# Six of eight memory-key slabs issued between the chunk inverse's levels and the state products, and RWKV's gate multiplied in by GpSimd

## The reference, cut to what matters

```python
y = wkv7_scan(rh, decay, kh, vh, -kk, kk * ah)       # 8 heads of 64, state 64 x 64 per head
y = head_group_norm(y, gn_w, gn_b, GN_EPS_RWKV)      # per head and token
bonus = jnp.sum(rh * kh * r_k, axis=-1, keepdims=True) * vh
return (y + bonus) * g                               # g: the gate
...
x = x + concat([y_ret, y_rwkv]) @ w_out
k, v = jnp.split(rmsnorm(mem, norm_mem) @ w_kv, 2, axis=-1)   # memory: 256 tokens
```

## Time and profile before

| | us |
|---|---|
| median of 3 runs (1261.39 to 1266.18) | 1261.75 |
| profiled execution, span | 1263.4 |
| TensorE (PE) busy | 1228.3 |
| VectorE (DVE) busy | 681.6 |
| ScalarE (ACT) busy | 552.0 |
| GpSimd (POOL) busy | 530.2 |

### The profile page before, as it was taken

One profiled execution on the slowest core, in us unless ns is written; L12 is line 12 of the kernel. 1 busy time (PEld: TensorE's weight loads), 2 busy tenths in 40 slices (PEclk: granted clock), 3 DMA queues, 4 the chain that ended last, 5 costly groups with the idle time before them and its releaser, 6 DMA issues.

```text
span 1263.4 us, 20863 instructions
## 1 busy us (share of the span) xinstructions
PE 1228.3 (97%) x8361; PEld 994.7 (79%) x8361; DVE 681.6 (54%) x821; ACT 552.0 (44%) x749; POOL 530.2 (42%) x245
## 2 busy tenths in 40 slices
PE   9999999877999999999999999999999999999997
PEld 5887777777878877888888888888787777887876
DVE  8877558776595432463152141344678765443832
ACT  5444553434534333532132231235343478885342
POOL 4333327303576422744444444446443332333453
PEclk9999999999999999999999999999999999999998
DMA  7552212100373210323332233222422421122231
GB/s 266 187 167 85 67 63 72 53 4 5 103 232 101 82 52 34 117 84 100 100 100 88 96 101 100 100 88 96 155 87 84 124 69 64 54 67 71 96 100 67
DMA packets 35099, 119.40 MB, mean 95 GB/s; under 512 B 4544, under 2 KB 4800, under 8 KB 34624
## 3 DMA queue, kind: packets, MB, share of 16 engines
q1 hardware_dynamic: 30624, 106.19, 25.2%
q10 hardware_dynamic: 4384, 11.93, 3.0%
HBM read 110.50 MB, written 2.10 MB: 89 GB/s over the span
## 4 chain that ended last, share of the span: by engine, by line
PE 82%; DVE 11%; ACT 3%; issue 3%; DMA 0%; POOL 0%; DVEq 0%; POOLq 0%; SPq 0%; ACTq 0%
PE banks L1455 22%; PE banks L1457 22%; PE banks L1456 22%; PE banks L1950 1%; PE banks L1966 1%; PE banks L2064 1%; PE banks L2049 1%; DVE a_lo L877 1%; DVE vv L869 1%; DVE yk L869 1%; PE banks L1478 1%; PE banks L1524 1%; PE banks L1480 1%; PE banks L1479 1%; DVE a_lo L869 1%
## 5 line engine op out<-in xcount | busy, mean ns | idle before, releaser
L386 POOL TENSOR_TENSOR w_lo<-w_raw,w_hi 128x1024 fp32r<-128x1024 f32 x144 | 352.0, 2445 | 509.4 <-ACT w_hi L443 509.3
L443 ACT ACTIVATE w_hi<-w_raw 128x1024 fp32r<-128x1024 f32 x144 | 152.7, 1061 | 318.5 <-PE banks L1457 213.5
L1457 PE MATMUL banks<-a_hi,w_lo 128*128 128x512 f32 x608 | 237.1, 390 | 0.0
L1455 PE MATMUL banks<-a_hi,w_hi 128*128 128x512 f32 x576 | 228.6, 397 | 1.8 <-DVE a_lo L869 1.8
L1456 PE MATMUL banks<-a_lo,w_hi 128*128 128x512 f32 x576 | 224.4, 390 | 0.0
L1457 PE MATMUL banks<-b_hi,w_lo 128*128 128x512 f32 x384 | 149.5, 389 | 0.0
L869 DVE TENSOR_TENSOR x_res<-banks,x_res 128x512 f32<-128x512 f32 x62 | 42.9, 691 | 177.7 <-PE banks L1457 174.2
L1457 PEld LDWEIGHTS banks<-a_hi,w_lo 128*128 128x128 f32 x608 | 114.2, 188 | 24.2
L386 POOL TENSOR_TENSOR w_lo<-w_raw,w_hi_mlp 128x1024 fp32r<-128x1024 f32 x36 | 87.3, 2424 | 109.1 <-ACT w_hi_mlp L443 109.1
L1455 PEld LDWEIGHTS banks<-a_hi,w_hi 128*128 128x128 f32 x576 | 108.2, 188 | 30.3 <-issue 4.9
L1456 PEld LDWEIGHTS banks<-a_lo,w_hi 128*128 128x128 f32 x576 | 108.3, 188 | 21.4 <-issue 0.2
(11 more groups left out here) (392 smaller groups left out, 2332.4 us busy)
## 6 DMA issues: line engine op xcount, KB each, us to landing
w_raw<-in_weights SPq DMA_DIRECT2D x188, 512.0 KB, 3.3
x_in<-in_x SPq DMA_DIRECT2D x4, 512.0 KB, 7.8
decay<-in_decay ACTq DMA_DIRECT2D x1, 2048.0 KB, 7.7
rot<-raw SPq DMA_DIRECT2D x32, 64.0 KB, 2.7
x_res<-in_x ACTq DMA_DIRECT2D x4, 512.0 KB, 4.4
consts<-in_consts SPq DMA_DIRECT2D x1, 1093.0 KB, 11.8
q_twice<-q_twice ACTq DMA_DIRECT2D x8, 128.0 KB, 2.8
k_stack<-qk_lo ACTq DMA_DIRECT2D x8, 128.0 KB, 2.6
```

The source lines that it names most:

```text
L386: nc.gpsimd.tensor_tensor(o, a, b, op).then_inc(S(name), 1)
L443: return nc.scalar.activation(o, a, f, **kw)
L1455: mm(o, high[:, w], hi[:, kc, :], start=kc == first, stop=False)
L1457: done = mm(o, w_lo[:, s % 4, w], hi[:, kc, :], start=False, stop=kc == last)
```

## The change

TensorE runs key slabs 0 to 3 after the `next_x` of levels 0 to 3, slab 4 after `chunk_states` and slab 5 after `transitions` (`memory_slab`), slabs 0 to 4 into bank 7 and slab 5 into bank 0. To free bank 7, two f share a pair of banks in the levels (`level_pair`, `level_place`), the transposes go to banks 4, 5, 6 and 4 (`turn_bank`), and `chunk_states(3)` shares banks with f = 2. ScalarE copies each early slab unscaled to SBUF (`memory_taken`); VectorE scales the six later, after `mem_v`. Slabs 2 and 3 have w_hi slots of their own (`w_hi_early`). The splits of the memory and of the slabs move ahead to match.

GpSimd multiplies the gate into the biased bonus (behind w_lo of slab 3) and into the RWKV output (behind w_lo of value slab 1); ScalarE scales by gn_w in its copy; VectorE adds the two (`gated_bonus`). The head sums come after slab 7, the spreads after value slabs 2 and 3. `mixer_lo` of the retention half moves ahead, and the first two W_OUT slabs run their first four chunks before either runs its last four.

```diff
 # GpSimd, behind w_lo of slab s
+                if s == S_MK + 3:
                     for f in range(NF):
-                        pool.wait_ge(S("r_copied"), f + 1)
-                        mul(QT[:, f, :], QT[:, f, :], rx[:, f, :], "qt_ready", ALU.add)
+                        pool.wait_ge(S("bonus_biased"), f + 1)
+                        mul(bon[:, f, :], bon[:, f, :], gx[:, f, :], "rwkv_gated")
+                if s == S_MK + 4:
                     for kc in range(1, KC):
...
+                if s == S_MK + 5:
+                    for f in range(NF):
+                        pool.wait_ge(S("r_copied"), f + 1)
+                        mul(QT[:, f, :], QT[:, f, :], rx[:, f, :], "qt_ready", ALU.add)
+                if s == S_MV + 1:
+                    for f in range(NF):
+                        pool.wait_ge(S("head_sq_ready"), NF + f + 1)
+                        mul(yk[:, f, :], yk[:, f, :], gx[:, f, :], "rwkv_gated")
 # ScalarE
+            def memory_taken(k):
+                act.wait_ge(S("slab_done"), S_MK + k + 1)
+                actv(mem_raw(k), early_bank(k), copy).then_inc(A("tile_taken"), 1)
...
+            for kc in range(KC):
+                memory_hi(kc)
             for lv in range(4):
+                if lv > 0:
+                    memory_taken(lv - 1)
                 for f in range(NF):
                     turned(NF * (lv + 1) + f)
-                memory_hi(2 * lv)
-                memory_hi(2 * lv + 1)
+                split_hi(S_MK + 2 + lv)
+                if lv in (1, 2):
+                    bonus_bias(2 * lv - 2)
+                    bonus_bias(2 * lv - 1)
...
-                actv(yk[:, f, :].rearrange("p (t u c) -> p u t c", u=2, c=CH), y, copy).then_inc(A("act_step"), 1)
+                actv(yk[:, f, :].rearrange("p (t u c) -> p u t c", u=2, c=CH), y, copy, scale=V("gn_w", f)).then_inc(A("act_step"), 1)
...
+            for c in range(KC):
+                split_hi(S_MV + 2 + c)
...
+            for f in range(NF):
+                act.wait_ge(S("y_ready"), f + 1)
+                actv(a_hi[:, NF + f, :], yk[:, f, :], copy).then_inc(A("a_hi_ready"), 1)
 # VectorE
                 for f in range(NF):
-                    dve.wait_ge(S("nx_done"), NF * lv + f + 1)
-                    tt(turned_slots(ak_tile(f, 0)), chunks(pair(f)), mask, ALU.mult).then_inc(D("px_ready"), 1)
+                    dve.wait_ge(S("nx_done"), NF * lv + 2 * (f // 2) + 2)
+                    tt(turned_slots(ak_tile(f, 0)), chunks(level_pair(f)), mask, ALU.mult).then_inc(D("px_ready"), 1)
...
-                if 1 <= lv < 4:
-                    memory_lo(2 * lv - 2)
-                    memory_lo(2 * lv - 1)
+                if lv == 0:
+                    for kc in range(KC):
+                        memory_lo(kc)
...
+            for c in range(NF):
+                mixer_lo(c)
             dve.wait_ge(S("mem_rms"), 1)
             recip(mem_rs[:], mem_rs[:]).then_inc(D("dve_step"), 1)
-            for n in range(KC):
+            for n in range(EARLY, KC):
...
+            for f in range(NF):
+                head_norm2(f)
+            gated_bonus(0)
+            gated_bonus(1)
+            mixer_lo(NF)
+            gated_bonus(2)
+            mixer_lo(NF + 1)
+            gated_bonus(3)
+            mixer_lo(NF + 2)
+            mixer_lo(NF + 3)
...
+            for k in range(EARLY):
+                step(tt(mem_k[:, k, :], mem_raw(k), mem_rs[:], ALU.mult))
 # TensorE
             for lv in range(4):
                 for f in range(NF):
-                    pe.wait_ge(S("px_ready"), NF * lv + f + 1)
+                    pe.wait_ge(S("px_ready"), NF * lv + 2 * (f // 2) + 2)
                     pe.wait_ge(S("xt_ready"), NF * lv + f + 1)
                     x_px(f)
                 for f in range(NF):
                     pe.wait_ge(S("xn_ready"), NF * lv + f + 1)
-                    turn(f, 2 * f)
+                    if lv == 0 or f == NF - 1:
+                        pe.wait_ge(S("xt_ready"), NF * (lv + 1) + 1 if f == NF - 1 else NF)
+                    turn(f, turn_bank(NF + f))
                 for f in range(NF):
-                    pe.wait_ge(S("xt_ready"), NF * (lv + 1) + f + 1)
+                    pe.wait_ge(S("xn_ready"), NF * lv + 2 * (f // 2) + 2)
                     next_x(f)
+                memory_slab(lv)
...
+            memory_slab(4)
             for f in range(NF):
-                pe.wait_ge(S("bc_ready"), f + 1)
+                pe.wait_ge(S("bc_ready"), f + 1 + (f == 2))
...
+            pe.wait_ge(S("r_copied"), 1)
+            memory_slab(5)
...
+            pe.wait_ge(S("heads_normed"), 3 * NF)
+            for n in range(2):
+                begin(S_WOUT + n)
+                part(S_WOUT + n, a_hi, a_lo, range(NF), "a_lo_ready" if n == 0 else None, KC)
+            for n in range(2):
+                part(S_WOUT + n, a_hi, a_lo, range(NF, KC), "a_lo_ready" if n == 0 else None, KC).then_inc(S("slab_done"), 1)
+            for n in range(2, KC):
+                slab(S_WOUT + n, a_hi, a_lo)
```

More of the change, by code:

```diff
@@ L324, in state, with mem_raw, early_bank, level_pair @@
             return ak_tile(f, 0)[:, 0, 0, :] if c == 1 else ST[:, c, f, :]
+        def mem_raw(k):
+            return mem_first[:, k, :] if k < 2 else mem_next[:, k - 2, :]
+        def early_bank(k):
+            return psum[EARLY_BANK[k]][:, 0:MEM]
+        def level_pair(f):
+            return pair(f // 2, f % 2)
+        def level_place(r, half, n, f):
+            return place(2 * (f // 2) + r, half, n, f % 2)
+        def turn_bank(n):
+            return 2 * n if n < NF else TURN_BANK[n % NF]
+        def state_pair(f):
+            return pair(2, 1) if f == NF - 1 else pair(f)
         def solved(f, u):
@@ L1722, in next_x @@
                                 r, t = slice(CH * p, CH * p + CH), 2 * tp + u
[L1723 removed]
+                                last = mm(level_place(p, u, 2 * h + tp, f), ABR[r, f, h, t, 0, :], X[r, f, h, t, :], start=True, stop=True)
                 last.then_inc(S("nx_done"), 1)
@@ L1764, in chunk_states @@
                             r = slice(CH * p, CH * p + CH)
-                            mm(place(2 * f + p, h, t), ABR[r, f, h, t, 2, :], GH[r, 2 * f + h, t, 1, :], start=True, stop=False)
+                            mm(place(bank + p, h, t, k), ABR[r, f, h, t, 2, :], GH[r, 2 * f + h, t, 1, :], start=True, stop=False)
                     for p in range(2):
@@ L1768, in chunk_states @@
                             r, e = slice(CH * p, CH * p + CH), (2 * f + h) * HD
-                            last = mm(place(2 * f + p, h, t), k_tok[r, t, e:e + HD], v_tok[r, t, e:e + HD], start=False, stop=True)
+                            last = mm(place(bank + p, h, t, k), k_tok[r, t, e:e + HD], v_tok[r, t, e:e + HD], start=False, stop=True)
                 last.then_inc(S("bc_done"), 1)
@@ L1779, in transitions, with memory_slab @@
                             last = mm(o, GH[r, 2 * f + h, t, 0, :], ABR[r, f, h, t, 1:3, :], start=True, stop=True)
-                last.then_inc(S("at_done"), 1)
+                last.then_inc(S("bc_done"), 1)
+            def memory_slab(k):
+                s, o = S_MK + k, early_bank(k)
+                high = hi_slot(s)[0]
+                pe.wait_ge(S("w_lo_ready"), s + 1)
+                if 0 < k < 5:
+                    pe.wait_ge(S("tile_taken"), S_MK + k)
+                for kc in range(KC):
+                    if k == 0:
+                        pe.wait_ge(S("mem_lo_ready"), kc + 1)
+                    w = slice(kc * P, (kc + 1) * P)
+                    mm(o, high[:, w], mem_hi[:, kc, :], start=kc == 0, stop=False)
+                    mm(o, high[:, w], mem_lo[:, kc, :], start=False, stop=False)
+                    last = mm(o, w_lo[:, s % 4, w], mem_hi[:, kc, :], start=False, stop=kc == KC - 1)
+                last.then_inc(S("slab_done"), 1)
             def y_inputs(f):
@@ L1941, in slab_and_sums @@
                 part(s, b_hi, b_lo, range(KC - 2, KC), "b_lo_ready", KC * k).then_inc(S("slab_done"), 1)
-            for n in range(KC):
-                slab(S_WOUT + n, a_hi, a_lo, "a_lo_ready" if n == 0 else None, KC)
+            pe.wait_ge(S("heads_normed"), 3 * NF)
[6 more added lines that the diff above has]
+                slab(S_WOUT + n, a_hi, a_lo)
             def xscores(h):
```

131 lines of the change are left out of this document (69 added, 62 removed).

## The result

| | before | changed |
|---|---|---|
| median of 20 runs each, us | 1263.38 (1260.14 to 1266.18) | 1265.30 (1262.96 to 1267.25) |
| ratio, 95% interval | | 1.0018 [1.0011, 1.0025] |
| the same pair on a second chip, us | 1264.41 (23 runs) | 1264.03 (12 runs), 1.000 [0.9986, 1.0013] |
| profiled execution, span, us | 1263.4 | 1264.8 |

The change costs 0.18% on the first chip and nothing on the second: no difference of 0.5%, as the likeliest case had it, but on the other side of no change (+1.9 us where -1.9 was forecast), and 0.3 us above the range.

A forecast was written before the change was run, and what follows sets the result against it. TensorE, carrying 82% of the last chain, was the bound, so only its waits could be won. Running shift: +13.8 us by `y_inputs`, -6.3 after slabs 6 and 7, -6.1, -3.6 at W_OUT slab 2, +1.7 clock: -1.9, 1259.9; range 1253 to 1265.

The forecast's parts named there:

- the likeliest case: The prediction's main forecast for the whole kernel: 1259.9 us, 0.15% faster, a change of -1.9 us; chance 0.50.
- first level: First level of the chunk inverse: 10.6 us against a 10.0 period, because its `next_x` lies in a half-clock stretch.
- half clock behind it: After the wait at W_OUT slab 2: one more 3.4 us stretch at half clock, 1.7 us lost; bounds 0 and 3.4.
- covered: First level: eight `memory_lo` on VectorE, 4.3 us, delay the mask multiplications but lie under TensorE's `next_x` and slab 0.
- The fetch stalls: Instruction packets limit small-matmul runs: one `x_px` block in the levels stalls 0.65 us, two in `chunk_states` 2.9 in all.
- The end wait: TensorE before W_OUT slab 2 waits 5.1 us for VectorE's first `x_res` addition; slab 2 starts at 381.5 instead of 385.1.
- ScalarE's late a_hi: Before W_OUT slab 2: ScalarE copies a_hi of yk behind all eight `split_hi`, a_hi(4) at 366.0, starting VectorE's chain late.
- off the path: GpSimd's eight gate multiplications, about 1.4 us each, four in the levels and four at 337 to 343, don't lengthen the path.
- against 1: Rival 1: no end wait, VectorE reaching `x_res` by 376.4; -8.7 us, 1253; chance 0.15.
- against 2: Rival 2: clock falls in the levels, 1.7 us each; in all four +4.9 us, 1266.7; chance 0.12.
- against 3: Rival 3: the slabs' slow matmuls let instruction blocks arrive ahead, so fetch stalls vanish; -5.4 us, 1256.3; chance 0.13.
- Rival 4: Slabs fill no idle time in the levels; `rn_ready` (+1.4) and longer VectorE chain eat later gains; +0.5, 1262; chance 0.10.

The follow-up runs named there:

- changed_again: The changed kernel run again without edits, on another chip beside the kernel before: 1264.03 us against 1264.41, ratio 1.000.
- memory_lo_alone: Changed kernel with ScalarE's split of early key slab 2 moved from the first level to the second: 0.9981 of the kernel before.
- fetch_probe_4: Kernel before with 512 64-column and 512 128-column 64x64 matmuls of blank data ahead, on four quadrants: 128 records issue in 1.87 us, next begin after 3.45 or 3.73.
- a_hi_between_splits: Changed kernel with ScalarE copying a_hi of y two at a time behind its seventh and eighth value-slab splits: 0.9997 of the kernel before.
- keys_scaled_late: Changed kernel with VectorE's six early-key scalings moved from ahead of the first x_res sum to among the sums: 1260.11 us, 0.9951 of the kernel before.
- thin slabs: Changed kernel with each of the six early key slabs keeping 3 of its 24 matmuls: 1260.68 us in one run.

## Why the prediction missed

The steps, each as the prediction gave it and as the profiled execution of the changed kernel had it. The error is counted at W_OUT slab 2, start 385.76 against 381.5, and behind the half clock.

| step | forecast | measured | error |
|---|---|---|---|
| first level | 10.6 | 13.18 | +2.6 |
| level period | 10.0, once +0.65 | 10.02, 10.03, one stall of 0.3 without effect | -0.65 |
| last `next_x` | no stall | stall of 1.2 | +1.2 |
| from `last_xt` over `y_inputs` to key slab 6 | states 13.3, two stalls in the chunk states | states 13.9 | +1.1 |
| slabs 6 and 7, head sums | 7.3 | 7.56 | +0.3 |
| value slabs | 23.3 | 23.64 | +0.3 |
| value slabs' end to slab 2 | 16.0, wait of 5.1 | 15.46, wait of 4.8 with its pacing | -0.5 |
| half clock behind it | 1.7 lost | 6.8 us of it, 2.3 lost | +0.6 |

The sum is +4.9, and -1.9 + 4.9 = +3.0 is the shift of every slab from 52 on (+2.9). The tail of the kernel before had a half-clock stretch more at 1252.7, which gives 1.5 back: spans 1263.4 and 1264.8. This is the account of one execution, and 0.9 us of it lay ahead of the first `turn` (248.8 against 247.9). In changed_again the span of the stages is 143.1 us, as in the kernel before (143.0), with the same first level and the same end wait; it had half the half clock and shorter fetch stalls.

**The step that failed** is "covered": that the eight `memory_lo`, priced at 4.3 us, would lie under `next_x` and slab 0. They took 6.7, because GpSimd subtracts slab 2 in the middle of them; moved apart they took 4.6 and the level 11.3 (memory_lo_alone), 1.9 us of the 2.6. That much, two fifths of the miss, was in the forecast's own rows: it had read that a VectorE instruction with two SBUF inputs waits out GpSimd's, used it for the gate, and not for `memory_lo`, which has two SBUF inputs too. The Trainium skill, page "SBUF — State Buffer" (SBUF: two separate sides), says that the one that comes second of such a pair is blocked until the first has finished; 2.09 us more beside a 2.37 us subtraction agrees with it. Most of the rest is fetch stalls, below. The forecast also gave the 0.6 over 10.0 to a half clock, which in this execution had fallen at 233.4, ahead of the change.

**The fetch stalls** were counted on from one stall of the trace before, block by block. The mechanism is right (fetch_probe_4), the count was good for the chunk states (two stalls at 1.0 and 1.7) and missed the one in the last `next_x`. Its size isn't fixed by the kernel: from start to start that stall was 0.9 to 1.2 us in six of the nine profiled executions with the early slabs in full and below 0.6 in the other three, with the same order on TensorE.

**The end wait** was right in place, releaser and size: `x_res`, 5.1 forecast, 4.8 from start to start. The forecast also had what sets it: "the first waits for w_lo of slab 2", at 12.5 us behind the value slabs where it was 11.9. Its story of ScalarE's late a_hi ahead of that had no part: a_hi_between_splits moved the a_hi and gained 0.2 us, changed_again had it later and lost nothing, and keys_scaled_late moved the scalings and gained all of the wait but 0.9. That it brings a half-clock stretch was right as well: the six profiled executions with a wait of 4.2 to 4.4 us there have a stretch that starts at 379 to 384, the six without it have none.

**The gate** "off the path" was wrong for the kernel before (0.9977 alone), where VectorE's gate stood ahead of `a_lo` and its 1.8 us. In the changed kernel the traces give it 1.1 us, which the ratios can't show.

**The rivals.** The end wait was there (against 1). The clock didn't fall in the levels (against 2); with thin slabs it fell in the first one, within a wait of 4.3 us. The fetch stalls didn't vanish (against 3). Rival 4 came nearest in its time (+0.5), by other ways: `rn_ready` cost 0, and the time lay in the first level.

## What to carry to other kernels

When work is moved ahead into idle time of the bound engine, look at what stays behind in its old place: here six small scalings, 4.9 us on an engine busy for 54% of the span, stood ahead of the one sum that frees a bank, waited for GpSimd there, and ate what the six moved slabs had won. Price VectorE work with two SBUF inputs by what GpSimd does at that moment, on every such instruction, the moved ones first. Then ask what pins the late work: making ScalarE's copies early won nothing, since the scalings waited for a subtraction that came when it did. And test the parts of a change alone and together, and read them in the trace at their own place: the gate seemed worth 0.2%, nothing or 0.3% by the ratios, and 1.1 and 1.3 us by the windows.

## What the runs showed of the hardware

- **Instruction stream.** Runs of 64x64 matmuls of 64 columns on four quadrants pass 128 records (256 instructions with the weight loads; one 16 KB packet in about as long, 7 in 29 us) in 3.45 to 3.73 us, though they issue in 1.87. The first 261 records of the run passed without a gap. On two quadrants they take as long by themselves and don't stall; with 128 columns the stalls are 0.24 us at most. The Trainium skill, page "Runtime: NRT & Kernel Launch" (Instruction fetch mechanics), calls the crossing mostly hidden; for these runs the measurement decides, and it is not.
- **The half clock behind a wait varies.** The same 4.4 us wait was followed by 6.8 us at 1.2 GHz in one execution of the changed kernel and by 3.4 in another; the granted clock of 380 to 387 us was 0.76 in the latter.
- **A scaling beside a subtraction.** In six profiled executions VectorE's scalings (two SBUF inputs, 128x256, 0.42 us alone) stand beside GpSimd's w_lo of 2.4 to 2.6 us: the one that meets it ends 0.3 us behind it, in all six, after up to 2.6 us.
